# Ten landing places for streamed weights, the lower halves written over the landed chunks

## The reference

```
u = rms_norm(x, norm_mix_g) @ w_in                    # both mixers' inputs
x = x + concat([ssd_mixer(u[:SSD_IN]), rwkv7_mixer(u[SSD_IN:])]) @ w_out
x = x + cross_attention(rms_norm(x), rms_norm(mem), wq, wk, wv, wo)
x = x + square(relu(rms_norm(x) @ ffn_w1)) @ ffn_w2
mod = silu(c) @ ada_w + ada_b                         # 2048 x 12288, one or two rows of input
h = rms_norm(x) * (1 + scale) + shift
q, k, v, f, hy = split(h @ w_in_2)
x = x + g1 * (merge(attention, fourier, hyena) @ w_out_2)
x = x + g2 * (gelu(conv(h2 @ w_gate)) * (h2 @ w_up)) @ w_down
out = rms_norm(x)
```

## Time and profile before

| | |
|---|---|
| median of 3 runs | 3231.94 us (3230.67 to 3234.11) |
| profiled execution | 3229.23 us |
| its span in the trace | 3227.4 us |
| PE busy / PEld busy | 3089.8 / 2696.5 us |
| DVE / ACT / POOL busy | 1917.2 / 1415.5 / 244.4 us |
| bytes moved by DMA | 620.07 MB |

### The profile page before, as it was taken

How to read it: one execution, slowest core, us unless ns; L and a number is a source line. 1 busy time by engine, 2 the same in 40 slices (tenths; PEclk the granted TensorE clock), 3 DMA queues, 4 the chain that set the end, 5 groups by cost and what they waited for, 6 DMA issues and landing times.

```text
span 3227.4 us, 54438 instructions
## 1 busy us (share of the span) xinstructions
PE 3089.8 (96%) x22670; PEld 2696.5 (84%) x22670; DVE 1917.2 (59%) x2598; ACT 1415.5 (44%) x1994; POOL 244.4 (8%) x203
## 2 busy tenths in 40 slices
PE   7999989899999999999999999999998999999998
PEld 6898978787888888888788889988877888888887
DVE  5475763543755785555555565345667666666666
ACT  4343442433544573444434454343425445444443
POOL 1100321020100110000000230010001000000002
PEclk9999999999999999999999999999999999999999
DMA  6554555546644666777777777763434566656654
GB/s 213 177 159 132 156 177 198 189 157 207 228 153 148 205 191 191 230 253 241 256 246 253 249 242 239 252 187 115 159 104 147 173 205 182 187 180 194 187 177 146
DMA packets 535783, 620.07 MB, mean 192 GB/s; under 512 B 19451, under 2 KB 459926, under 8 KB 534177
## 3 DMA queue, kind: packets, MB, share of 16 engines
q1 hardware_dynamic: 527008, 586.51, 57.7%
q0 software_dynamic: 3344, 23.78, 2.1%
q10 hardware_dynamic: 5184, 6.29, 0.6%
HBM read 608.12 MB, written 8.39 MB: 191 GB/s over the span
## 4 chain that ended last, share of the span: by engine, by line
PE 78%; DVE 4%; ACT 2%; DMA 2%; issue 1%; POOL 0%; SPq 0%; ACTq 0%; DVEq 0%; POOLq 0%
PE psum L591 35%; PE psum L592 18%; PE psum L563 3%; PE psum L566 3%; PE psum L565 3%; PE psum L691 3%; PE psum L1749 2%; PE psum L625 2%; PE psum L627 2%; PE psum L628 2%; DVE wlo L520 1%; DMA wraw<-in_ffn_w 1%; PE psum L675 1%; PE psum L2398 0%; PE psum L1940 0%
## 5 line engine op out<-in xcount | busy, mean ns | idle before, releaser
L513 ACT ACTIVATE whi<-wraw 128x1024 fp32r<-128x1024 f32 (+1 forms) x948 | 977.7, 1033 | 1203.7 <-PE psum L592 455.4
L520 DVE TENSOR_TENSOR wlo<-wraw,whi 128x1024 fp32r<-128x1024 f32 (+1 forms) x948 | 1150.8, 1226 | 559.6 <-ACT whi L513 552.6
L591 PE MATMUL psum<-g,whi 128*128 128x512 f32 x2816 | 1000.9, 397 | 15.8 <-issue 8.2
L591 PE MATMUL psum<-h,whi 128*128 128x512 f32 x2240 | 793.4, 396 | 5.0 <-DVE h L2037 2.4
L592 PE MATMUL psum<-g,wlo 128*128 128x256 f32 x2816 | 788.3, 280 | 0.0
L591 PEld LDWEIGHTS psum<-g,whi 128*128 128x128 f32 x2816 | 530.5, 188 | 162.9 <-issue 25.9
L592 PE MATMUL psum<-h,wlo 128*128 128x256 f32 x2240 | 633.6, 283 | 0.0
L592 PEld LDWEIGHTS psum<-g,wlo 128*128 128x128 f32 x2816 | 530.7, 188 | 0.5
L591 PEld LDWEIGHTS psum<-h,whi 128*128 128x128 f32 x2240 | 421.2, 188 | 122.9 <-issue 21.9
L592 PEld LDWEIGHTS psum<-h,wlo 128*128 128x128 f32 x2240 | 421.7, 188 | 0.2
L563 PE MATMUL psum<-h,whi 128*128 128x256 f32 x1040 | 304.3, 293 | 35.1 <-DVE h L896 22.0
(11 more groups left out here) (468 smaller groups left out, 3368.2 us busy)
## 6 DMA issues: line engine op xcount, KB each, us to landing
wraw<-in_ffn_w SPq DMA_DIRECT2D x256, 512.0 KB, 6.7
wraw<-in_w_in SPq DMA_DIRECT2D x204, 512.0 KB, 4.7
wraw<-in_ada_w SPq DMA_DIRECT2D x192, 512.0 KB, 4.8
wraw<-in_ffn_w_up SPq DMA_DIRECT2D x160, 512.0 KB, 4.5
wraw<-in_w_out SPq DMA_DIRECT2D x64, 512.0 KB, 4.5
wraw<-in_ffn_w_down SPq DMA_DIRECT2D x64, 512.0 KB, 4.6
wraw<-in_xattn_wk SPq DMA_DIRECT2D x32, 512.0 KB, 4.5
wraw<-in_xattn_wv SPq DMA_DIRECT2D x32, 512.0 KB, 4.6
```

The source lines that it names most:

```text
L513: e.activation(high(i), view(WRAW[i % NR], i), ACT.Copy).then_inc(*hi.up(i))
L520: e.tensor_tensor(low(i), view(WRAW[i % NR], i), high(i).bitcast(F32), SUB).then_inc(*lo.up(i))
L591: e.matmul(both_of(g, j), w_hi[:, kk, s:s + 128], X[:, k, :], start=k == 0, stop=False, skip_group_check=True)
```

## The change

The constant `NR` goes from 6 to 10. The lower halves get no memory of their own any more: `WLO` is laid over `WRAW` (the ten landing places are allocated, their scope is closed, and ten `wlo` tensors of another type are allocated at the same addresses). DVE's subtraction so reads a landed chunk and writes its lower half into the same place. The memory is 14 tiles of 4 KB per partition as before: 10 places and 4 upper halves, where it was 6, 4 and 4.

A place is now occupied until TensorE has finished its chunk, split or plain. So SP waits, for chunk i, until TensorE has finished chunk i - 10 (before: for the lower half of chunk i - 6, or for TensorE's use of it where it is plain). DVE's own wait for TensorE before a lower half goes; the wait for the upper half stays.

```
-NR = 6
+NR = 10
...
-        WRAW = [new(f"wraw{i}", [P, CS]) for i in range(NR)]
+        landing_places, place = scope()
+        WRAW = [place(f"wraw{i}", [P, CS]) for i in range(NR)]
+        landing_places.close()
+        WLO = [new(f"wlo{i}", [P, CS], F32R) for i in range(NR)]
         WHI = [new(f"whi{i}", [P, CS], F32R) for i in range(NH)]
-        WLO = [new(f"wlo{i}", [P, CS], F32R) for i in range(NH)]
...
+        def raw(i):
+            return view(WRAW[i % NR], i)
...
         def low(i):
-            return view(WLO[nth[i] % NH], i)
+            return view(WLO[i % NR], i)
...
         def split_lo(e, i):
             if i not in plain:
                 e.wait_ge(*hi.at(i))
-                if nth[i] >= NH:
-                    e.wait_ge(*mm.at("chunk", halved[nth[i] - NH]))
-                e.tensor_tensor(low(i), view(WRAW[i % NR], i), high(i).bitcast(F32), SUB).then_inc(*lo.up(i))
+                e.tensor_tensor(low(i), raw(i), high(i).bitcast(F32), SUB).then_inc(*lo.up(i))
...
             for i in range(len(chunks)):
                 j = i - NR
-                if j in plain:
+                if j >= 0:
                     e.wait_ge(*mm.at("chunk", j))
-                elif j >= 0:
-                    e.wait_ge(*lo.at(j))
-                e.dma_start(view(WRAW[i % NR], i), chunks[i][0]).then_inc(*w_in[i % NR].up())
+                e.dma_start(raw(i), chunks[i][0]).then_inc(*w_in[i % NR].up())
```

More of the change, by code:

```diff
@@ L512, in split_hi @@
                     e.wait_ge(*mm.at("chunk", halved[nth[i] - NH]))
-                e.activation(high(i), view(WRAW[i % NR], i), ACT.Copy).then_inc(*hi.up(i))
+                e.activation(high(i), raw(i), ACT.Copy).then_inc(*hi.up(i))
         def split_lo(e, i):
@@ L691, in ada_p @@
                             x = e.matmul(PSUM[32 * q:32 * q + 32, ada_bank(n), :], SF[:, k:k + 16, :].rearrange("p k m -> p (k m)"),
-                                         view(WRAW[(i if q > 1 else before) % NR], i)[:, q % 2, :], start=k < 4, stop=k >= 12)
+                                         raw(i if q > 1 else before)[:, q % 2, :], start=k < 4, stop=k >= 12)
                         ends = [("chunk", before), ("chunk", i)]
```

## The result

| | before | after |
|---|---|---|
| median | 3231.94 us (5 runs, 3224.83 to 3239.20) | 3201.09 us (5 runs, 3199.47 to 3202.67) |
| ratio | | 0.9904, 95% interval 0.9887 to 0.9921 |
| span of the trace | 3227.4 us | 3200.8 us |

The account below looks back on a forecast made before the run. TensorE, busy 3089.8 of 3227.4 us, was taken to bound the kernel, leaving its idle and low-clock time to win. Terms 27 + 11 - 4 + 0 + 0 + 2 = 36 us gave 3196 us, range 3183 to 3225.

Parts of the forecast that it names:

- SP and ACT: From 393 to 824 us, SP's transfers start four chunks earlier; ACT's waits for landings fall from 150 us to under 20.
- Rival C: Landings were hidden, each chain wait having a second reason almost as late: 0 to 4 us gained, about 3230; chance 0.06.
- Idle time given back: Four short stretches between 420 and 793 us hold 30.35 us of TensorE idle time; 27 us of it goes.
- rival B: Serial ACT and DVE steps behind a landing bind anyway, in the first woven stretch: 13 us gained, 3219; chance 0.26.
- L1464 would end well before: Near 439 us, DVE's step would end before TensorE wants it, with ACT's step at 413.64 some 7 us earlier.
- The clock: In the first woven stretch's idle spots, low granted clock loses 14.1 us of full-speed time; 11 us counted as gain.
- The moved upper halves: In the first woven stretch, one of two ACT upper halves stands earlier: a 4 us loss, bounds 0 to 45.
- Rival D: ACT's moved upper halves wait for TensorE, which waits for side steps behind them: 7 us slower, 3239; chance 0.08.
- In place: DVE's subtraction in place reads and writes as much as before, its dropped wait was redundant: 0 us.
- The start: Four more 512 KB transfers queued early might delay x: bounds 0 to 7 us, taken as 0.
- Second and third woven stretch: Three short TensorE waits in the 3.8 us idle from 1340 to 2105 us could go: 2 us gained.
- Elsewhere: From 824 to 1340 us chunks are early anyway, upper halves wait for TensorE, not landings: no gain, same length.

Follow-up runs that it names:

- old waits: Changed kernel with its ten places and in-place lower halves, but SP's waits and the cap on ACT's order as before the change: 3232.57 us, ratio 0.9993.
- old order of ACT alone: Changed kernel with only the cap on how early ACT's upper halves stand put back to its old value: 3201.33 us, ratio 0.9898.
- eight places: Changed kernel, but SP waits for TensorE's end of chunk i - 8, so two of the ten places stay unused: 3204.22 us, ratio 0.9905.
- hold at 110: Changed kernel, but SP issues no transfer after chunk 109 until two small RWKV loads on GpSimd's queue have landed: 3193.04 us, ratio 0.9877.
- RW = 1.0: Changed kernel with SP held before chunk 110 for two small loads, and the RWKV side steps' weight raised from 0.92, so they come earlier: 3206.14 us.

## Why the prediction was right, step by step

**SP and ACT.** Right in kind: the gain is SP's new wait and nothing else (old waits: 3232.57 us, old order of ACT alone: 3201.33). The figure for what ACT's waits would fall to, under 20 us, was wrong: 49.8 us. The step that failed is "ACT's 150 us of waiting for landings should be nearly gone": that sum is no lever. With eight places it was 133.5 us at nearly the same time, with ACT's old order 15.1 us at just the same time. What counts is whether TensorE waits. Rival C is out by the time itself: the landings were not hidden.

**Idle time given back.** Mis-sized: 27 us forecast, 18.3 measured (39.2 to 20.9). I expected TensorE's idle time under 15 us. The step that failed is "Behind each stands an ACT instruction queued behind an L513 that waits for a landing". The waits of 3.49, 3.42 and 3.09 us went, and three of 2.0 us for lower halves with them, but not all the others did. Behind 600 us, 1.66 and 1.94 us stand at a lower half and at a GpSimd step, as 1.51 and 1.94 did before, and 1.68 us stand at L1745, where 2.85 us were, now without a wait for another engine in the trace. The small load adds 2.1 us.

At L1732 (L1736 now) 3.0 of the 5.13 us stay, and this is rival B at work. Counted from the first matmul of the stretch, the DVE step that TensorE waits for began at 52.2 us before and at 48.1 us after. TensorE was ready for it at 48.4 us and at 46.4 us. The chain came 4.2 us earlier and TensorE 2.0, so 2.2 us of waiting went. The late small load is not the reason that the rest stayed. With the load on time (hold at 110) the DVE step begins at 44.2 us, another 3.8 us earlier, and TensorE is ready at 42.5 us, also 3.8 us earlier; it waits as long as after:

```profile
434.34 0.70 PE L1736 MATMUL psum<-mats,rld 128*128 128x128 f32 x4 [2.97 <-DVE rk L1468]
```

So "L1464 would end well before" the time at which TensorE wants it was wrong: it took the chain's gain and left TensorE where it had been.

**The clock.** Right: 11 us forecast, 10.3 us measured in the stretch, for the same matmuls. That the two are so close is in part luck. TensorE's busy time in the stretch was 398.5 and 402.7 us in the two traces with old waits, and 388.2 and 391.2 us in the two of the changed kernel, so the gain by clock was 7 to 14 us, depending on the pair. The idle time was steadier: 39.2 and 40.1 us, then 20.9 and 19.3.

**The moved upper halves.** 4 us forecast, none measured (3201.33 with the old order, 3201.09 and 3197.79 with the new). In the stretch after, ACT waits for TensorE at its upper halves for 12.8 us, where D wanted over 60. Rival D is out for this change. It was no empty rival: one place fewer in the ring of upper halves costs 56 us by the medians, most of it outside this stretch.

**In place.** 0, right. **The start.** 0, right: holding chunks 6 to 9 brought nothing. The bound of 7 us was not needed. The Trainium skill, "DMA: Bandwidth & Descriptors", section "Queues, rings and completion order", has each DMA engine go round its queues; the start agrees, since x is no later by more than the traces differ (TensorE's first matmul at 22.02 us before, 22.26 after, and 22.49 with chunks 6 to 9 held). But taking turns is not the same as being undisturbed: the load of rkt on GpSimd's queue took 5.1 instead of 3.0 us with SP's next two chunks beside it. I had weighed the deeper queue only at the start, and this is where it cost something, 3.6 us at that place.

**Second and third woven stretch.** 2 us forecast, 3.0 measured from 1340 to 1898 us of before, and these 3 us are missing when only the first stretch has the new wait. **Elsewhere** no gain, right to 0.01 us over 516 us.

Added up: 18.3 + 10.3 + 3.0 = 31.6 us. The trace's own difference of 26.6 us is this less 3.7 us before the stretch and 1.3 us behind 1870 us. Two traces of the changed kernel differ by 1.7 and 5.7 us in these two parts. The medians give 30.9. The forecast of 36 had 9 too much in the idle time and 4 too much against it, two errors of opposite sign, so the total came out nearer than its terms. Rival B took no more than a part: it is what holds the remaining 3.0 us at L1736, and what makes `RW = 1.0` slower.

## What to carry to other kernels

If a landing place is held by the slowest user of the data, look at the place in the stream where that user is farthest behind. Six places were too few in the first woven stretch, and enough in the 516 us behind it, which ten places did not shorten. Rewriting data where it landed gave the depth for no memory and no measurable time. Judge such a change by the busiest engine's idle time and clock, not by the waits of the engine that feeds it, which went from 150 to 134, 50 or 15 us for nearly the same gain. When the stream of weights runs deeper, look for the small loads on other queues that the chain waits for. Letting one go first gave the lowest median here, though its worth is not settled, and holding eight transfers for it instead of four gained nothing. And when a chain is freed, ask how much earlier the engine that waits for it will come as well.

## What the runs showed of the hardware

*A small load beside a deeper stream.* 192 KB on GpSimd's queue took 3.0 us to its use with SP's queue held, and 5.1 us with two chunks of 512 KB issued around it (3.0 us in six traces, 4.6 to 5.1 us in six others).

*A DVE step beside GpSimd.* Lower halves, 1.22 us as a rule, took much longer where they began during an element-wise step of GpSimd. Kernel after, DVE and GpSimd in order of time:

```profile
418.87 3.08 DVE L524 TENSOR_TENSOR wlo<-wraw,whi 128x1024 fp32r<-128x1024 f32 x1 [0.47 <-ACT whi L519]
```

```profile
418.48 2.38 POOL L1363 TENSOR_TENSOR rk<-rk 128x1024 f32<-128x1024 f32 x1 [23.95 <-DVE rrt L1450]
```

GpSimd's step ended at 418.48 + 2.38 = 420.86 us; DVE's ended at 421.95 us, 1.09 us later, about what it needs alone. So by this row DVE was not slowed but held until GpSimd was done. It is so in the second half too:

```profile
626.30 3.39 DVE L524 TENSOR_TENSOR wlo<-wraw,whi 128x1024 fp32r<-128x1024 f32 x1
```

```profile
625.20 3.40 POOL L1368 TENSOR_TENSOR ric<-ric,rkk 128x1024 f32<-128x1024 f32 x1 [9.61 <-DVE rkk L1458]
```

GpSimd ended at 628.60 us and DVE at 629.69, again 1.09 us later. The Trainium skill, "SBUF — State Buffer", section "Who interferes with whom", says that a DVE instruction with two inputs in SBUF and a GpSimd instruction that reads SBUF exclude each other; these rows agree. The first stands right ahead of the reciprocal that L1736 waits for, and takes 1.9 us more there than alone. That does not make it the cause of TensorE's wait: with ACT's old order the same lower half stands behind GpSimd's step and takes 1.23 us, and yet TensorE waits 4.4 us at L1736, and the kernel takes 3201.33 us.

```profile
420.34 1.23 DVE L524 TENSOR_TENSOR wlo<-wraw,whi 128x1024 fp32r<-128x1024 f32 x1 [2.80 <-ACT whi L519]
```

*Traces of one kernel differ.* The kernel with the old waits and the kernel before agree in their medians to 0.9 us beside each other (3232.57 and 3233.47), but their traced executions are 10 us apart at the end of the first woven stretch (834.05 and 824.01 us), with 0.95 and 0.96 as clock there. Two traces of the changed kernel have spans of 3200.8 and 3194.8 us. So a difference of a few us in one place counts only where several traces share it, as for the small load, and for the second woven stretch: 558.2 to 558.9 us in the three traces with old waits there, 555.2 to 555.8 in all others.
